# Weight splits moved up at the head of two stages, the last gate closed ahead of them, and head sums moved behind the mix, in a two-block model on one core

## What is computed

```python
# end of the state-space mixer: "gating stage"
g = jax.nn.gelu(y); val, gate = jnp.split(g @ w_glu, 2, axis=-1)
x = x + val * jax.nn.sigmoid(gate)
# end of an FFN layer: "side gates"
gate = jax.nn.sigmoid(rms_norm_2(x, ple_norm[i]) @ ple_w_gate[i])
x = x + gate * (p[i] @ ple_w_proj[i])
# second attention
k, v = shared_kv(x, kv_norm, kv_w, k_norm)
q = rms_norm_2((rms_norm_2(x, attn_norm) @ w_q).reshape(b, l, 8, 2, 64), q_norm)
pm = softmax(q @ k + bias); attn = pm[:, :, 0] - lam * pm[:, :, 1]
x = x + rms_norm_2(attn @ v, subln) * (1 - lam_init) @ w_o
```

## Time and profile before

| | |
|---|---|
| median of 3 runs | 2021.35 us (2021.18 to 2023.01) |
| profiled execution | 2024.65 us, its span 2022.8 us |
| mean granted PE clock | 0.985 |
| PE busy | 1968.0 us, 97% |
| PE weight loads | 1597.5 us, 79% |
| DVE busy | 1218.0 us, 60% |
| ACT busy | 806.4 us, 40% |
| POOL busy | 445.3 us, 22% |
| chain that ended last | PE 87%, DVE 8%, ACT 2% |

### The profile page before, as it was taken

One profiled execution on the slowest core, in us unless ns is written; L12 is line 12 of the kernel. 1 busy time (PEld: TensorE's weight loads), 2 busy tenths in 40 slices (PEclk: granted clock), 3 DMA queues, 4 the chain that ended last, 5 costly groups with the idle time before them and its releaser, 6 DMA issues.

```text
span 2022.8 us, 26418 instructions
## 1 busy us (share of the span) xinstructions
PE 1968.0 (97%) x9622; PEld 1597.5 (79%) x9622; DVE 1218.0 (60%) x1713; ACT 806.4 (40%) x1280; POOL 445.3 (22%) x625
## 2 busy tenths in 40 slices
PE   7999999999999998999999999999989999999998
PEld 7999678888888786877887877777767777878887
DVE  4445456474544896466556466744677766475565
ACT  4322333122224685344324234544565444243343
POOL 3020029998844472100000001100000200000010
PEclk9999899999999999999999999999889999999999
DMA  4221023254452352222322323332211123223232
GB/s 149 82 90 64 32 84 97 91 196 156 174 203 93 112 170 64 94 73 93 115 73 93 115 73 125 95 94 84 58 58 53 53 94 113 75 92 115 73 125 94
DMA packets 66227, 201.62 MB, mean 100 GB/s; under 512 B 6550, under 2 KB 19350, under 8 KB 66124
## 3 DMA queue, kind: packets, MB, share of 16 engines
q1 hardware_dynamic: 57372, 166.39, 24.8%
q0 software_dynamic: 8752, 33.84, 4.9%
HBM read 184.44 MB, written 15.77 MB: 99 GB/s over the span
## 4 chain that ended last, share of the span: by engine, by line
PE 87%; DVE 8%; issue 2%; ACT 2%; POOL 1%; DMA 0%; SPq 0%; DVEq 0%; POOLq 0%; ACTq 0%
PE ps L454 62%; PE ps L591 7%; PE ps L1771 7%; PE ps L742 2%; PE ps L1906 2%; DVE w_lo L433 1%; PE ps L817 1%; PE ps L443 1%; PE ps L2021 1%; DVE rstd L571 1%; PE ps L773 1%; DVE t L1433 1%; PE ps L2043 1%; POOL t L535 0%; DVE t L2056 0%
## 5 line engine op out<-in xcount | busy, mean ns | idle before, releaser
L433 DVE TENSOR_TENSOR w_lo<-raw,w_hi 128x1024 fp32r<-128x1024 f32 x308 | 398.8, 1296 | 159.7 <-ACT w_hi L429 159.1
L454 PE MATMUL ps<-x_hi,w_hi 128*128 128x512 f32 x1152 | 458.8, 398 | 3.7 <-DVE w_lo L433 2.6
L454 PE MATMUL ps<-x_lo,w_hi 128*128 128x512 f32 x1152 | 455.5, 395 | 0.0
L454 PE MATMUL ps<-x_hi,w_lo 128*128 128x512 f32 x1152 | 453.5, 394 | 0.0
L429 ACT ACTIVATE w_hi<-raw 128x1024 fp32r<-128x1024 f32 x308 | 322.3, 1049 | 235.1 <-DMA raw<-in_wstream 134.4
L454 PE MATMUL ps<-a_hi,w_hi 128*128 128x512 f32 x704 | 278.6, 396 | 3.3 <-DVE w_lo L433 3.3
L454 PE MATMUL ps<-a_hi,w_lo 128*128 128x512 f32 x704 | 278.5, 396 | 0.0
L454 PE MATMUL ps<-a_lo,w_hi 128*128 128x512 f32 x704 | 278.4, 395 | 0.0
L535 POOL TENSOR_TENSOR t<-t,sq 128x512 f32<-128x512 f32 x49 | 72.9, 1488 | 926.2 <-ACT sq L526 924.6
L454 PEld LDWEIGHTS ps<-x_hi,w_hi 128*128 128x128 f32 x1152 | 216.4, 188 | 68.9 <-issue 11.3
L454 PEld LDWEIGHTS ps<-x_hi,w_lo 128*128 128x128 f32 x1152 | 216.7, 188 | 49.6
(11 more groups left out here) (414 smaller groups left out, 2964.5 us busy)
## 6 DMA issues: line engine op xcount, KB each, us to landing
raw<-in_wstream SPq DMA_DIRECT2D x308, 512.0 KB, 3.2
ev<-mix_ev POOLq DMA_DIRECT2D x16, 512.0 KB, 4.6
mix_cp<-c_p POOLq DMA_DIRECT2D x8, 640.0 KB, 3.4
cp<-mix_cp POOLq DMA_DIRECT2D x8, 640.0 KB, 5.4
mix_ev<-v_b POOLq DMA_DIRECT2D x8, 512.0 KB, 3.5
fall<-fall POOLq DMA_DIRECT2D x4, 544.0 KB, 4.6
h<-in_xT SPq DMA_DIRECT2D x4, 528.0 KB, 6.3
mix_ev<-e_r POOLq DMA_DIRECT2D x1, 2048.0 KB, 9.9
```

Source lines behind the costliest of these rows:

```text
L433: e.tensor_tensor(w_lo[:, u.slot, :], raw[:, u.c % 2, :], w_hi[:, u.slot, :], ALU.subtract)\
L454: last = e.matmul(ps[:, bank, :], wt[:, u.slot, w], x[:, k0 + k, 0:SEQ], start=(k == 0 and n == 0), stop=(k == kt - 1 and n == 2))
```

## The change

Four edits. In the gating stage, the fifth unit (`U_GLU + 4`) is split ahead of gate 0 instead of after it; the sixth stays at m = 1. In `side`, DVE no longer runs `then` and the sixth `a_lo` ahead of the last gate: the last gate's multiply and add come first, and `then` and the last three `after` follow. `then` is called twice, with 0 in front of these and with 1 ahead of the last of them, so that the fourth unit `U_Q + 3` is split inside `side` too, ahead of the last `a_hi`/`a_lo`, and no longer in `attention2_first`. In `attention2`, the head sums of steps 2 and 7 stand behind the mix and the turned operand.

```diff
@@ side @@
-                if then and m == KT:
-                    then()
-                if after and m > lag:
+                if after and lag < m < KT:
                     after(m - 1 - lag)
...
-        if then and who == "act":
-            then()
+        if then:
+            then(0)
         if after:
-            for m in range(KT - lag, KT):
+            for m in range(KT - lag - (who == "dve"), KT):
+                if then and m == KT - 1:
+                    then(1)
                 after(m)
@@ attention2_first @@
-                    split_hi(e, Unit(U_Q + 3))
...
-                    split_lo(e, Unit(U_Q + 3))
@@ attention2, DVE @@
+                if 1 <= i < 33:
+                    dve_mix(i - 1)
+                turns(i, turn_dve, 1 if i < 36 else 0)
                 if done and done[0] == "group" and done[1] == 4 and done[2] % 4 == 3:
                     for tb in (done[2] // 4 * 2, done[2] // 4 * 2 + 1):
                         head_sums_dve(e, 4, tb)
-                if 1 <= i < 33:
-                    dve_mix(i - 1)
-                turns(i, turn_dve, 1 if i < 36 else 0)
@@ gating stage, ACT @@
+            if m != 1:
+                split_ahead(e, u if m else u.ahead(2), split_hi)
             if m:
-                split_ahead(e, u, split_hi)
                 split_ahead(e, u.ahead(1), split_hi)
@@ calls of side @@
-        side(e, "act", 0, U_GATEA, 5, attn_form, 2, lambda: split_hi(e, Unit(U_Q + 2)))
+        side(e, "act", 0, U_GATEA, 5, attn_form, 2, lambda n: split_hi(e, Unit(U_Q + 2 + n)))
@@ gating stage, DVE @@
+            if m == 0:
+                final_form(0)
+            if m != 1:
+                split_ahead(e, u if m else u.ahead(2), split_lo)
             if m:
-                split_ahead(e, u, split_lo)
                 split_ahead(e, u.ahead(1), split_lo)
-            else:
-                final_form(0)
```

More of the change, by code:

```diff
@@ L2561, in _ @@
              lambda m: x_dve(e, 5, m, "attn_norm", hi=a_hi, lo=a_lo), 2,
-             lambda: split_lo(e, Unit(U_Q + 2)))
+             lambda n: split_lo(e, Unit(U_Q + 2 + n)))
         c = COL["lambdas"]
```

## The result

| kernel | median, us | runs, us | ratio to before, 95% interval |
|---|---|---|---|
| before | 2021.35 | 2021.02 to 2025.79 (5) | |
| changed | 2009.42 | 2006.85 to 2013.15 (5) | 0.9935 [0.9924, 0.9947] |

The change gains 11.9 us between the medians and 13.1 us by the ratio (0.0065 x 2021.35). Forecast were 14.0 us and 2007.3; the median is 2.1 us above that and inside the range of 2003.0 to 2013.5. The profiled executions took 2024.65 and 2006.85 us, spans of 2022.8 and 2005.0: 17.8 us apart, more than the medians.

What follows compares the result with a forecast made beforehand. PE (TensorE), busy for 97% of the span, was taken as the bound. Gains of 4.9 + 3.4 + 4.8 + 3.7 = 16.8 us, less 1.8 and 1.0, left 14.0: 2021.35 - 14.0 = 2007.3 us, range 2003.0 to 2013.5.

Steps and rivals of the forecast that it cites:

- Gating stage: Fifth gating unit: splitting it ahead of the sigmoid removes PE's 3.27 us stall on w_lo; gain 4.9 us.
- Third and fourth unit: Second attention: PE's wait moves from fourth to third unit, 2.7 us late in all instead of 6.1; gain 3.4 us.
- The 0.3 and 0.4 us behind it: Second attention: further lateness after the third unit's w_lo, 0.3 us at a_lo and 0.4 at the fourth unit's w_lo.
- Rival A: Second attention's third and fourth unit: DVE gets in ahead of POOL, returning 6.1 us there; 2001.9 us in all; chance 0.10.
- Step 2: Head sums behind the mix: qr_lo comes 1.8 us sooner and 3.0 us of low clock go; gain 4.8 us.
- if the clock then holds: Second attention's step 2: condition that PE's remaining 1.9 us idle time does not lower the clock, worth 3.0 us.
- The correction of 1.8 us: Taken off the sum: remaining 1.9 us idle times at third unit and step 2 may lower the clock; half of 3.6.
- a stall costs about twice its idle time: PE's four listed stalls: matmuls behind each start every 0.43 us instead of 0.23, at the lower clock.
- Step 7: Head sums behind the mix: kr_lo comes 2.1 us sooner; 5.0 us, limited by DVE to a gain of 3.7.
- Rival B: Second attention: later stalls grow, so both head-sum steps return half or nothing; gain 5 to 10 us, about 2013; chance 0.20.
- rival E: Second attention: fourth head sum ends after 1442.30, delaying ACT's square and the exponentials; slower, above 2025.4 us; chance 0.02.
- rival D: All four stalls: the clock gives nothing back and only idle time returns, 7.8 us, 2013.5; chance 0.06.

Runs made afterwards that it cites:

- e1: Kernel before with only the gating stage's fifth unit split early; 2018.69 us against 2022.64, ratio 0.9978.
- e2: Kernel before with only the last side gate and the second attention's third and fourth unit reordered; 2020.99 us, ratio 0.9991 to before.
- e4: Changed kernel with POOL's last two adds of the token sum held until DVE has the fourth unit's w_lo; 2014.22 us, ratio 0.9958 to before.
- e7: Changed kernel with the last two adds of the token sum done by DVE instead of POOL, behind its last a_lo; 2004.20 us, ratio 0.9914 to before.
- e9: Changed kernel with the head sums of step 2 alone put back ahead of the mix; 2010.45 us, ratio 0.9934 to before.
- e6: Changed kernel with the head sums of step 7 alone put back ahead of the mix; 2012.59 us, ratio 0.9953 to before.
- e5: Changed kernel with DVE's turned operands (qr_lo, kr_lo) moved ahead of the mix; 1997.70 us, ratio 0.9874 to before.
- e10: Changed kernel measured once more, unaltered, on another chip; 2006.73 us, ratio 0.9914 to before.
- e3: Kernel before with only the head sums of steps 2 and 7 moved behind the mix; 2016.16 us, ratio 0.9965 to before.

## Why the prediction was right

**1. Gating stage, 4.9 forecast, 4.7 to 4.95 measured** (e1 and the table). The new wait was put at 0.15 at most, and at 0.2 in the sum; it is 0.20. The table load behind the split is 1.28 us and the sigmoid follows 0.02 behind it. The Trainium skill, "ScalarE: Activation LUTs", section "What ACT_TABLE_LOAD costs", adds a drain of 1.38 us, and no run here shows it at this switch.

**2. Third and fourth unit, 3.4 forecast, 3.3 measured** without a low stretch (e2) and 2.55 with one. Every step of the layout came out, at 5.56 us earlier: w_lo of the third unit ends at 1299.86 (1305.4 forecast), the first a_lo at 1301.56 (1307.1), w_lo of the fourth at 1303.35 (1308.9). PE waits 1.88 us (2.0). The 0.3 and 0.4 us behind it show in e2, not as idle time but in the starts: 0.44 + 0.33 us where two steps take 0.46 (a_lo), 0.54 + 0.34 where they take 0.46 (w_lo). Rival A, 6.1 us, is refuted by the product's 1.83 us, and e4 and e7 show POOL's last two adds as the cause of 1.1 us of the wait. The 0.8 that remain are not shown to be DVE's own queue, for the add ahead of the product stayed in both runs and stretches it by 1.83 - 0.68 = 1.15 us. My estimate is that without that add w_lo would be in time: 1.15 is more than 0.8, and ACT has w_hi ready at 1300.38 in e4, before DVE would ask for it. No run moved it. A low stretch there was put at 1.8 us; it cost 521.84 - 521.08 = 0.8. The explanation is read from the rows and not tried: while PE runs slowly, a_lo and w_lo of the fourth unit catch up, and the 0.3 + 0.4 us are not paid. In the changed kernel the two matmuls in question start 0.42 us (at the low clock) and 0.24 us behind the ones before them, with nothing on top.

**3. Step 2, 4.8 forecast, 3.2 measured** (e9). This is the term that was mis-sized. Its idle part was right (1.8 forecast, 3.74 to 1.94 measured); "if the clock then holds" was not: the remaining 1.94 us still brought the clock down, 0.83 where I had 1.00. The correction of 1.8 us for such a stretch in the sum describes what happened: 4.8 - 1.8 = 3.0. I had taken it once, between none and both; both profiled executions of the changed kernel, and e6 and e9, had both stretches, e2 and e5 did without the one at the third unit.

The trace of the kernel before could have told me that short waits bring the clock down, which the prediction called not shown by its rows. Windows that begin near the wait of 2.45 us ahead of the gating stage and near those of 1.71 and 1.45 us at later turns, with the columns of the earlier trace rows:

```profile
764.00:772.00 8.00, 5.55 (x38) 4.94 (x37) 7.66 (x12) 6.32 (x18) 4.86 (x9) 1.00 0.01 3
1474.00:1484.00 10.00, 8.29 (x34) 6.61 (x33) 6.07 (x18) 4.41 (x13) 0.54 (x1) 0.66 0.24 59
1508.00:1518.00 10.00, 8.55 (x37) 6.75 (x36) 5.14 (x17) 4.16 (x14) 0.54 (x1) 0.66 0.15 47
```

The waits of 1.71 and 1.45 us are followed by 0.66, and the one of 2.45 us by 1.00. So "a stall costs about twice its idle time" held for the four stalls that I had picked and is no rule for all.

**4. Step 7, 3.7 forecast, 3.7 measured** (e6), with 0.29 us left at step 8 (0.3), and a new wait of 0.88 at step 10, where DVE could not follow: that is why 5.0 was cut to 3.7. Rival B, which had all of attention give back 4 us and more, would have shown waits growing from step 10 on by over 3 us; they grew by 0.88. For rival E: the fourth sum ended at 1430.62, ACT's square began at 1431.27, 0.65 us later (0.6 forecast).

**The sum.** Forecast 14.0; 13.9 in the edited stages of the profiled pair, 13.3 by the three parts, 13.1 by the ratio of the first measurement and 17.4 (0.0086 x 2024.7) by that of e10. Nothing is left for rival D: 7.8 us of idle time do not explain any of these. Part of the agreement is luck: executions of one kernel on one chip lie 6.3 us apart for the changed kernel and 11.1 us for e1, and the changed kernel's two measurements give 13.1 and 17.4 us.

What stays open: why the same wait of 1.71 us is followed by a clock of 0.66 in e3, 0.83 in the changed kernel and 1.00 in e4. No run was made for that.

## What to carry to other kernels

Price a wait of the bounding engine with the clock behind it, as a range and not as a rule: in e5 4.45 us less of waiting returned 8.7 us, but the same wait of 1.71 us was followed by 0.66, 0.83 or 1.00. When one thing is moved out of the way of a late operand, look at what else still stands ahead of it on that engine: the head sums gave 6.6 us, and the mix, one line further on, another 8.7. Before an engine is held back for another's sake, see what the other does next without a gap: e4 moved 1.1 us of waiting into 4.88.

## What was not expected of the hardware

POOL and DVE shut each other out in both directions, and not always by who asks first. In the changed kernel a POOL add that asked at 1299.22, during w_lo, ran ahead of the a_lo of 1299.78, which took 1.77 us. The first of the two held adds of e4 did the same: it asked at 1305.76, during an a_lo, and DVE's small product behind that took 1.26 us. But the second add, which asked at 1307.66, 0.46 us before the second x_lo started, stood back for seven more of them and took 6.30 us. The Trainium skill, "SBUF — State Buffer", section "Who interferes with whom", says that issue order decides who blocks. The first two cases agree, the third does not, and no run here separates why.
